# A two-layer decoder trunk on one core: the second FFN product falls one group further behind the first

## What is computed

```
x = LN(ALPHA * x + attention(x))
up, gate = split(x @ w_in)              # w_in: 1024 x 5632
up = causal depthwise conv, width 3, over tokens (up) + conv_b
x = LN(ALPHA * x + (gelu(up) * gate) @ w_out)   # w_out: 2816 x 1024
```

## Time and profile before

| | us |
|---|---|
| median of 3 runs | 601.66 (601.48 to 602.28) |
| the profiled execution, its own time | 600.72 |
| its span in the profile | 598.4 |
| TensorE busy | 582.0 (97%) |
| DVE, ACT, POOL busy | 448.9, 335.1, 50.7 |
| mean granted TensorE clock | 0.994 |

### The profile page before, as it was taken

How to read it: one execution, slowest core, us unless ns; L and a number is a source line. 1 busy time by engine, 2 the same in 40 slices (tenths; PEclk the granted TensorE clock), 3 DMA queues, 4 the chain that set the end, 5 groups by cost and what they waited for, 6 DMA issues and landing times.

```text
span 598.4 us, 7752 instructions
## 1 busy us (share of the span) xinstructions
PE 582.0 (97%) x2720; PEld 474.0 (79%) x2720; DVE 448.9 (75%) x813; ACT 335.1 (56%) x560; POOL 50.7 (8%) x84
## 2 busy tenths in 40 slices
PE   8999999999999999999899999999999999999985
PEld 6887777788888888888688888877888888888864
DVE  4899994876887776667878897688678777666646
ACT  5766684245666545544545578934655555555520
POOL 5300001300000000000220003131000000000003
PEclk9999999999999999999999999999999999999998
DMA  8997865466788897766366955244858889777311
GB/s 305 292 327 242 257 190 187 135 203 188 223 271 285 272 284 217 213 226 203 121 210 193 335 177 193 90 140 121 266 177 264 257 251 299 229 245 245 106 35 70
DMA packets 95665, 127.86 MB, mean 214 GB/s; under 512 B 13404, under 2 KB 73612, under 8 KB 95628
## 3 DMA queue, kind: packets, MB, share of 16 engines
q1 hardware_dynamic: 94188, 123.19, 64.7%
q0 software_dynamic: 1152, 4.19, 2.1%
q10 hardware_dynamic: 288, 0.00, 0.0%
HBM read 108.23 MB, written 1.05 MB: 183 GB/s over the span
## 4 chain that ended last, share of the span: by engine, by line
PE 90%; DVE 5%; DMA 2%; ACT 1%; SPq 1%; issue 1%; DVEq 0%
PE wide L1280 17%; PE wide L1282 16%; PE wide L1281 16%; PE score L1282 6%; PE score L1280 6%; PE score L1281 6%; PE turn L1282 3%; PE turn L1280 3%; PE turn L1281 3%; PE outb L1282 3%; PE outb L1280 3%; PE outb L1281 3%; DMA kT<-turned 1%; DVE xT L990 1%; DVE w_lo L973 1%; DMA xs<-in_x 1%
## 5 line engine op out<-in xcount | busy, mean ns | idle before, releaser
L973 DVE TENSOR_TENSOR w_lo<-raw,w_hi 128x2048 fp32r<-128x2048 f32 (+1 forms) x120 | 210.6, 1775 | 65.9 <-ACT w_hi L786 65.9
L786 ACT ACTIVATE w_hi<-raw 128x2048 fp32r<-128x2048 f32 (+1 forms) x126 | 184.3, 1488 | 106.4 <-PE wide L1282 61.5
L1280 PE MATMUL wide<-w_hi,oT_hi 128*128 128x512 f32 x240 | 95.8, 399 | 5.8 <-DVE oT_lo L1215 5.8
L1281 PE MATMUL wide<-w_lo,oT_hi 128*128 128x512 f32 x240 | 94.2, 393 | 0.0
L1282 PE MATMUL wide<-w_hi,oT_lo 128*128 128x512 f32 x240 | 94.1, 392 | 0.0
L1280 PE MATMUL wide<-w_hi,xT 128*128 128x512 f32 x224 | 90.0, 402 | 0.3 <-DVE w_lo L1039 0.2
L1282 PE MATMUL wide<-w_hi,xT 128*128 128x512 f32 x224 | 87.5, 390 | 0.0
L1281 PE MATMUL wide<-w_lo,xT 128*128 128x512 f32 x224 | 87.3, 390 | 0.0
L1280 PE MATMUL score<-w_hi,xT 128*128 128x512 f32 x160 | 62.2, 389 | 0.0
L1281 PE MATMUL score<-w_lo,xT 128*128 128x512 f32 x160 | 62.2, 389 | 0.0
L1282 PE MATMUL score<-w_hi,xT 128*128 128x512 f32 x160 | 62.2, 389 | 0.0
(11 more groups left out here) (160 smaller groups left out, 848.0 us busy)
## 6 DMA issues: line engine op xcount, KB each, us to landing
raw<-in_ffn_w_in SPq DMA_DIRECT2D x88, 512.0 KB, 5.1
raw<-in_ffn_w_out SPq DMA_DIRECT2D x22, 1024.0 KB, 7.8
kT<-turned SPq DMA_DIRECT2D x104, 128.0 KB, 2.8
raw<-in_a_w_qkv SPq DMA_DIRECT2D x9, 1024.0 KB, 7.2
raw<-in_w_kv_shared SPq DMA_DIRECT2D x8, 1024.0 KB, 7.1
raw<-in_a_w_o SPq DMA_DIRECT2D x4, 1024.0 KB, 6.7
raw<-in_b_w_q SPq DMA_DIRECT2D x4, 1024.0 KB, 5.0
raw<-in_b_w_o SPq DMA_DIRECT2D x4, 1024.0 KB, 5.2
```

What stands on the lines that cost most here:

```text
L786: ins = nc.scalar.activation(w_hi[c % RING][:, part], raw[c % RAW_RING][:, part], ACT.Copy)
L973: ins = nc.vector.tensor_tensor(w_lo[c % RING][:, part], raw[c % RAW_RING][:, part], w_hi[c % RING][:, part].bitcast(F32), ALU.subtract)
L1280: nc.tensor.matmul(dst, a_hi, b_hi, start=start, stop=False, skip_group_check=True)
L1281: nc.tensor.matmul(dst, a_hi, b_lo, start=False, stop=False, skip_group_check=True)
```

## The change

The second product of group i-3, not i-2, follows the first of group i, and in(10) is followed by two of them, out(7) and out(8). TensorE's order becomes in(0), in(1), in(2), in(3), out(0), in(4), out(1), ..., in(9), out(6), in(10), out(7), out(8), and the same tail. Chunk numbers, loads and splits follow from the new list `ffn_order`. In the last step the split of in(10)'s second chunk + 4 is now that of out(10)'s chunk, whole; the splits of out(7) + 4 and out(8) + 4 (next 0 and next 1 in layer 0, nothing in layer 1) are made by halves behind h_hi(10) and h_lo(10).

```
+    def second_behind(i):
+
+        if i == GROUPS - 1:
+            return [GROUPS - 4, GROUPS - 3]
+        return [i - 3] if i >= 3 else []
+
+    ffn_order = []
+    for i in range(GROUPS):
+        ffn_order += [(i, 0), (i, 1)] + [(n, 2) for n in second_behind(i)]
+    ffn_order += [(GROUPS - 2, 2), (GROUPS - 1, 2)]
+
     def ffn_chunk(layer, i, which):

-        base = layer * LAYER_CHUNKS + QKV_CHUNKS + WO_CHUNKS
-        if which == 2:
-            return base + (3 * i + 6 if i < GROUPS - 2 else 2 * GROUPS + i)
-        return base + (2 * i if i < 3 else 3 * i - 2) + which
-
-    def second_behind(i):
-
-        return [i - 2] if i >= 2 else []
+        return layer * LAYER_CHUNKS + QKV_CHUNKS + WO_CHUNKS + ffn_order.index((i, which))
...
@@ -924,13 +928,13 @@
                     else:
-                        split_hi(ffn_chunk(layer, i, 1) + RING, 0)
-                        split_hi(ffn_chunk(layer, i, 1) + RING, 1)
+                        split_hi(ffn_chunk(layer, i, 1) + RING)
                         taps(i)
                         make_gelu(i)
                         make_h_hi(i)
-                        split_hi(ffn_chunk(layer, i - 2, 2) + RING, 0)
-                        split_hi(ffn_chunk(layer, i - 2, 2) + RING, 1)
+                        for n in second_behind(i):
+                            split_hi(ffn_chunk(layer, n, 2) + RING, 0)
+                            split_hi(ffn_chunk(layer, n, 2) + RING, 1)
...
@@ -1241,14 +1245,18 @@
                     else:
-                        split_lo(ffn_chunk(layer, i, 1) + RING, 0)
-                        split_lo(ffn_chunk(layer, i, 1) + RING, 1)
+                        split_lo(ffn_chunk(layer, i, 1) + RING)
                         add_taps(i)
                         for tt in range(2):
                             make_hidden(i, tt)
                             make_h_lo(i, tt)
-                        if ffn_chunk(layer, i - 2, 2) + RING == SHARED:
-                            split_shared_lo()
+                        for n in second_behind(i):
+                            c = ffn_chunk(layer, n, 2) + RING
+                            if c == SHARED:
+                                split_shared_lo()
+                            else:
+                                split_lo(c, 0)
+                                split_lo(c, 1)
```

## The result

| | before | after |
|---|---|---|
| median of 4 runs | 601.97 us (601.48 to 603.27) | 592.92 us (592.33 to 593.44) |
| the profiled execution | 600.72 us, span 598.4 | 593.44 us, span 590.9 |
| TensorE busy | 582.0 us | 580.6 us |
| mean granted clock | 0.994 | 0.997 |

The ratio is 0.985 (95% interval 0.983 to 0.987): 9.05 us faster at the median, against 7.7 forecast (the kernel before was 601.97 us in this set and 601.66 in the one that the forecast started from). Between the two profiled executions it is 7.28 us.

What follows compares the result with a forecast made beforehand. PE bounds the kernel, busy 582.0 of 598.4 us. Gain 7.83 less 0.2 gives 7.6, taking the profiled 600.72 to 593.1; 0.94 carried on makes 594.0 us, range 592.0 to 596.5.

Steps and rivals of the forecast that it cites:

- The two waits: PE waiting for DVE's h_lo(10) in each layer's FFN tail; with slow matmuls, 7.83 us together, all to go.
- Part 1: FFN tail, both layers: out(7) in front gives 13.60 us of cover against 11.28, 2.3 us slack, so both waits go.
- Part 2: Layer 0's handover: next 0 split behind h(10); DVE arrives just as the residual's input does; cost 0, at most 1.2 us.
- Part 3: FFN beginning: chunk 10 split in step 3, slack 0.1 to 0.4 us in layer 0, about 1.2 in layer 1.
- the sum's 0.2 us: Cost allowed for chunk 10's late split at the FFN's beginning, subtracted from 7.83 us.
- likeliest case: Whole kernel: both waits gone, at most 1 us of new waits; 594.0 us (592.9 to 595.0), chance 0.70.
- rival 2: Clock paid twice: nine slow steps behind layer 0's wait too (1.68 us) in median runs; 592.2 us, chance 0.11.
- I count the slow matmuls once: Only layer 1's wait counted as followed by slow matmuls, 1.68 us; layer 0's clock was 1.00.
- the 0.94 us: Median of runs (601.66) above the profiled execution (600.72), unexplained, added unchanged to 593.1.
- the 16.4 us: PE time not busy in 598.4 us, taken as all that a change of order can bring.
- Rivals 3, 4 and 5: 3: 1 to 4 us taken back, chance 0.13; 4: tail wait stays, 0.03; 5: slower at chunk 10, 0.03.
- Rival 5: Chunk 10 in step 3, both layers: chain late by 6 us costs 10.5 against 7.8, 604.5 us; chance 0.03.

Runs made afterwards that it cites:

- the two experiments with extra DVE work: Changed kernel with one short, then two longer unused DVE instructions ahead of layer 0's last residual: 593.14 us, then 594.92 us.
- the same four DVE instructions: Four unused DVE instructions ahead of step 3's first turn, both layers: 598.37 us in the changed kernel, 602.22 in the kernel before.
- the trace at 0.990: Kernel before with four unused DVE instructions ahead of step 3's first turn in both layers; mean clock 0.990, measured 602.22 us.

## Why the prediction was right, and where it was off

- **The two waits** (3.20 and 2.95 us): gone, with nothing in their place. Right, by the trace to 0.01 us in layer 0.
- **Part 1, the chain of 11.28 us against 13.60 of cover:** right; 2.6 us of slack for 2.3.
- **Part 2, parity at the handover:** right. 1.56 us measured for 1.57, and the two experiments with extra DVE work show the path to be as tight as said, but for 0.2 to 0.3 us.
- **Part 3, chunk 10's slack of 0.1 to 0.4 us:** the sum's 0.2 us for it was not paid, the lo part was 0.4 us early. The mechanism is right (the same four DVE instructions cost 5.3 us in the kernel where chunk 10 is split in step 3 and nothing where it is split in step 2), and the slack, 0.56 us by that experiment in layer 0, was a little more than had been worked out.
- **The sum and the clock:** here the prediction was off, by 1.1 us in the time and by 1.4 in the gain (7.7 for 9.05). Its likeliest case reached down to 592.9, so 592.92 lies at its edge; that the range went lower is owed to rival 2. The step that failed is "I count the slow matmuls once", and with it the 0.94 us between profiled execution and median that was carried on as if it belonged to the measurement. It was more slow matmuls than one stretch: filling the waits brought 3.03 us where 1.68 had been counted, the clocks of 31 of 35 runs lie below that of the profiled one by about what a second stretch costs, and the trace at 0.990 has two. The profiled execution had one. That was rival 2, at a chance of 0.11; its own number, 592.2, is nearer to the result than the forecast's 594.0. The argument against it (the runs lie 0.76 to 1.56 us above the profiled execution, less than 1.68) asked for too exact a match in runs that differ by half a microsecond at their start. Nor were the 16.4 us in which TensorE was not busy all that could be gained: its busy time fell by 1.4 us too, since slow matmuls count as busy.
- **Rivals 3, 4 and 5:** the places named in 3 and 5 are the right ones, and both become waits as soon as something is added there (the extra DVE work in step 3 and at the handover) or the two-chunk step moves to the end. Rival 5's 604.5 should be 604.3 by its own sum (601.66 - 7.83 + 10.5).

## What to carry to other kernels

When the only wait of the bounding engine stands behind a chain of fixed length, put finished, independent work between the chain's start and its consumer, and look for the price where that work was taken from: here a step with less work for TensorE, in which the feeding engine falls behind. In this kernel such a step belongs where the feed has chunks of lead (the start of the stage) and not where a handover hangs on the same engine (its end): the same cover was worth 2.6 us less there at the median, 1.7 of them traced to the handover. And compare the profiled execution's clock and span with the other runs' before carrying their difference on as a constant.

## What the runs showed of the hardware

Behind TensorE's wait of 2.8 to 3.1 us between two dense stretches, matmul steps of 0.43 us instead of 0.227 follow in most executions, but not in all and not equally many. In four traces with six such waits there were none once (clock 1.00), eight or nine four times (0.62 in one of them, above) and fourteen once (0.50). The fall can show with the first matmul behind the wait or later, here as much as 0.76 us (three full-speed steps) and 1.23 us (five) into the next stretch. Filling the wait with idle matmuls kept the clock at 1.00 and was worth 3.03 us with the waits unchanged. Behind the shorter waits of these traces (1.27 and 2.02 us for chunk 10, 1.68 at the handover) no slow step was seen, in one execution each.

The Trainium skill, "TensorE: Matmul & The Clock Gate", section "Part 1: The HAM clock gate", says that the point at which the clock turns varies from run to run. These traces agree: behind layer 0's wait the slow steps began at once in one execution, 0.76 us later in another, and did not come in a third.
